# A two-layer decoder trunk on one core: other SBUF places for the operands of the split matmuls

## What is computed

```python
x = x + 0.5 * swiglu(rms_norm(x, ffn1_norm), w_gate, w_up, w_down)      # D_FF = 2816
h = rms_norm(x, mix_norm)
qa, ka, va, c_q, c_kv, k_r, g_a, g_b = split(h @ w_in)
o_a = swa_attention(qa, ka, va, ...)        # 8 heads of 64, window 128, (256, 512)
o_b = mla_attention(c_q, c_kv, k_r, ...)    # 8 heads, low-rank q and kv, (256, 512)
merged = sigmoid(g_a) * (o_a @ w_branch_a) + sigmoid(g_b) * (o_b @ w_branch_b)
x = x + merged @ w_out
x = x + 0.5 * swiglu(rms_norm(x, ffn2_norm), w_gate2, w_up2, w_down2)
```

## Time and profile before

| | |
|---|---|
| Median of 2 runs | 1044.32 us (1044.23 to 1044.41) |
| Profiled execution, whole | 1044.65 us |
| its span, first to last instruction | 1042.9 us |
| Instructions | 15577, of them 5656 matmuls |
| PE busy | 1038.1 us |
| PEld, DVE, ACT, POOL busy | 897.9, 718.1, 585.8, 62.6 us |
| Granted TensorE clock | 1.000 |
| Read from HBM | 186.04 MB, 179 GB/s over the span |

### The profile page before, as it was taken

One profiled execution on the slowest core, in us unless ns is written; L12 is line 12 of the kernel. 1 busy time (PEld: TensorE's weight loads), 2 busy tenths in 40 slices (PEclk: granted clock), 3 DMA queues, 4 the chain that ended last, 5 costly groups with the idle time before them and its releaser, 6 DMA issues.

```text
span 1042.9 us, 15577 instructions
## 1 busy us (share of the span) xinstructions
PE 1038.1 (100%) x5656; PEld 897.9 (86%) x5656; DVE 718.1 (69%) x1132; ACT 585.8 (56%) x935; POOL 62.6 (6%) x69
## 2 busy tenths in 40 slices
PE   9999999999999999999999999999999999999998
PEld 8888888998888888888888888889988888888887
DVE  6766666768786876666686666666688868676665
ACT  6555455466973754554565455455678646454552
POOL 1052000112100000000000000001211000000000
PEclk9999999999999999999999999999999999999999
DMA  6665544455435455655445555634454346545541
GB/s 264 244 221 185 212 167 166 135 185 183 156 122 202 162 190 192 206 185 208 178 148 205 201 184 184 210 131 151 162 202 162 121 162 220 203 161 201 191 171 61
DMA packets 35270, 187.60 MB, mean 180 GB/s; under 512 B 4497, under 2 KB 4641, under 8 KB 20129
## 3 DMA queue, kind: packets, MB, share of 16 engines
q1 hardware_dynamic: 34704, 186.03, 50.9%
q0 software_dynamic: 240, 0.53, 0.2%
q10 hardware_dynamic: 288, 0.54, 0.1%
HBM read 186.04 MB, written 1.05 MB: 179 GB/s over the span
## 4 chain that ended last, share of the span: by engine, by line
PE 99%; DMA 1%; DVE 0%; SPq 0%; ACT 0%; issue 0%
PE ps L1365 96%; PE ps L1786 1%; PE ps L1389 1%; DMA w_raw<-in_w_ffn 1%; PE ps L1815 1%; PE ps L1851 0%; PE ps L1695 0%; PE ps L1687 0%; DVE hT L1001 0%; PE ps L1413 0%; DVE x L994 0%; ACT w_hi L547 0%; SPq L312 0%; SPq L311 0%; DVE w_lo L912 0%
## 5 line engine op out<-in xcount | busy, mean ns | idle before, releaser
L1365 PE MATMUL ps<-hT,w_hi 128*128 128x512 f32 x1408 | 341.6, 391 | 0.3 <-DVE hT L1001 0.3
L1365 PEld LDWEIGHTS ps<-hT,w_hi 128*128 128x128 f32 x1408 | 259.1, 188 | 50.3 <-DVE hT L1001 0.5
L879 DVE TENSOR_TENSOR w_lo<-w_raw,w_hi 128x2048 fp32r<-128x2048 f32 x82 | 188.0, 2292 | 87.2 <-ACT w_hi L542 87.2
L1365 PEld LDWEIGHTS ps<-hT,w_lo 128*128 128x128 f32 x1408 | 180.8, 191 | 7.7 <-DVE w_lo L912 0.4
L1365 PE MATMUL ps<-hT,w_lo 128*128 128x256 f32 x1408 | 183.0, 283 | 0.0
L1365 PE MATMUL ps<-w_hi,hT 128*128 128x512 f32 (+2 forms) x576 | 174.1, 377 | 0.0
L542 ACT ACTIVATE w_hi<-w_raw 128x2048 fp32r<-128x2048 f32 x85 | 161.9, 1905 | 13.3 <-PE ps L1365 13.2
L1365 PE MATMUL ps<-w_lo,aTh 128*128 128x512 f32 x352 | 137.2, 390 | 0.0
L1365 PE MATMUL ps<-w_hi,aTl 128*128 128x512 f32 x352 | 137.0, 389 | 0.0
L1365 PE MATMUL ps<-w_hi,aTh 128*128 128x512 f32 x352 | 136.8, 390 | 0.0
L571 ACT ACTIVATE S<-ps 128x256 f32<-128x256 f32 x88 | 33.7, 383 | 159.7 <-PE ps L1365 159.7
(11 more groups left out here) (166 smaller groups left out, 958.2 us busy)
## 6 DMA issues: line engine op xcount, KB each, us to landing
w_raw<-in_w_ffn SPq DMA_DIRECT2D x85, 1024.0 KB, 5.0
w_raw<-in_w_ffn SPq DMA_DIRECT2D x92, 512.0 KB, 5.7
w_raw<-in_w_gate SPq DMA_DIRECT2D x16, 1024.0 KB, 4.9
w_raw<-in_w_proj SPq DMA_DIRECT2D x16, 592.0 KB, 4.7
w_raw<-in_w_branch SPq DMA_DIRECT2D x8, 1024.0 KB, 4.8
w_raw<-in_w_out SPq DMA_DIRECT2D x8, 1024.0 KB, 4.8
w_raw<-in_w_uq SPq DMA_DIRECT2D x4, 384.0 KB, 3.0
SG<-in_w_ffn SPq DMA_DIRECT2D x1, 1024.0 KB, 11.4
```

What stands on the lines that cost most here:

```text
L879: dve.tensor_tensor(wl_gu[b], raw_gu[b], wh_gu[b].bitcast(F32), ALU.subtract).then_inc(lo_gu.sem, 1)
L1365: return pe.matmul(dst, w, m, start=start, stop=stop, skip_group_check=True)
```

## The change

Rows of three tensors get holes, and three unused tensors stand between others, so that columns and tiles start at other byte addresses. In bytes: a column of hT goes from 2048 to 2080; a gap of 192 follows; a half of aTh takes 1280 in place of 1024; a gap of 320; a half of aTl takes 1184 in place of 1024; a gap of 192; a block of oTh and of oTl takes 1040 in place of 1024. The reads and writes cover the same elements as before. Where oTh and oTl were written as one run of 512 elements they are now written as two of 256. No instruction is added or removed.

```diff
+HT_GAP, OT_GAP = 8, 4
+AT_GAP, AT_GAP_L, ATH_GAP, ATL_GAP = 48, 80, 64, 40
...
         x = sb("x", [P, TT, D_MODEL])
-        hT = sb("hT", [P, KC, 2, SEQ], F32R)
+        hT_rows = sb("hT", [P, KC, 2 * SEQ + HT_GAP], F32R)
+        hT = hT_rows[:, :, 0:2 * SEQ].rearrange("p k (s n) -> p k s n", s=2)
         hTh, hTl = hT[:, :, 0, :], hT[:, :, 1, :]
-        aTh = sb("aTh", [P, 2, SEQ], F32R)
-        aTl = sb("aTl", [P, 2, SEQ], F32R)
+        aT_gap = sb("aT_gap", [P, AT_GAP])
+        aTh = sb("aTh", [P, 2, SEQ + ATH_GAP], F32R)[:, :, 0:SEQ]
+        aT_gap_l = sb("aT_gap_l", [P, AT_GAP_L])
+        aTl = sb("aTl", [P, 2, SEQ + ATL_GAP], F32R)[:, :, 0:SEQ]
+        oT_gap = sb("oT_gap", [P, AT_GAP])
         work = sb("work", [P, 4 * SEQ])
...
-        oTh = sb("oTh", [P, 8, SEQ], F32R)
-        oTl = sb("oTl", [P, 8, SEQ], F32R)
+        oTh = sb("oTh", [P, 8, SEQ + OT_GAP], F32R)[:, :, 0:SEQ]
+        oTl = sb("oTl", [P, 8, SEQ + OT_GAP], F32R)[:, :, 0:SEQ]
...
-                        act.activation(oTh[:, 4 * br + 2 * c:4 * br + 2 * c + 2, :].rearrange("p c n -> p (c n)"),
-                                       ps[:, c, :], ACT.Copy).then_inc(ot_hi.sem, 1)
+                        act.activation(oTh[:, 4 * br + 2 * c:4 * br + 2 * c + 2, :],
+                                       ps[:, c, :].rearrange("p (c n) -> p c n", c=2), ACT.Copy).then_inc(ot_hi.sem, 1)
...
-                        dve.tensor_tensor(oTl[:, part, :].rearrange("p c n -> p (c n)"), ps[:, c, :],
-                                          oTh[:, part, :].rearrange("p c n -> p (c n)").bitcast(F32),
-                                          ALU.subtract).then_inc(ot_lo.sem, 1)
+                        dve.tensor_tensor(oTl[:, part, :], ps[:, c, :].rearrange("p (c n) -> p c n", c=2),
+                                          oTh[:, part, :].bitcast(F32), ALU.subtract).then_inc(ot_lo.sem, 1)
```

## The result

The changed kernel takes 1060.24 us (median of 2 runs, both within 0.01 us) against 1044.32 before: a ratio of 1.0154, interval 1.0137 to 1.017. It is 16 us slower: less than 2%, but the whole interval lies above 1. The forecast was no change.

The account below looks back on a forecast made before the run. PE's matmul start-to-start distances were taken to bound the kernel. The 1042.9 us span plus 0 to 0.1 us, with the pitch term at 0, gave a forecast of 1044 us; the range ran from 1008 to 1062 us.

Parts of the forecast that it names:

- What bounds the kernel: PE, busy 1038.1 of 1042.9 us: the time is the sum of its matmuls' start-to-start distances.
- the 13.3 ns: Time per fp32r matmul beyond its columns, claimed whatever the length: 66.7 us over 5000, all that addresses could win.
- No added work, ACT and DVE at nothing: No instruction or wait added; the two-run writes of oTh and oTl taken as 0, bound 0.1 us.
- The pitch term: Effect of moved operand places on PE's 5000 fp32r matmuls: taken as 0, bounds 55 us faster to 16 us slower.
- The first test: Branch products with weights at 0 and oTh at 256 take 227 ns, like `down` with both at 0: displacement worth 0.
- The second test: Feed-forward stretches with DVE and ACT differently busy at wandering SBUF addresses: pitch 226 to 227 ns in both, so 0.
- rival A: Running matmul's reads collide with the next weight load's; separated places make it faster, 1014 or 994 us; over 2% faster: 0.26.
- Rival C: The 13.3 ns belong to swapping weights in the array: 1044 us, likeliest; shares 0.64 with the forecast.
- half gain: Half of the 13.3 ns goes: 4540 matmuls gain 6.7 ns, 30 us, 1014 us; 22 us without the 256-column ones.
- Rival B: An operand off a wide boundary costs an extra beat: 16 us at most, 1060 us; over 2% slower: 0.10.
- The sign for B: In the changed kernel's timeline, odd columns of hT would be slower than even ones; no size given.
- The sign for A: In the changed timeline, the distance of `down` falls first, while column 0 of hT keeps 227 ns.

Follow-up runs that it names:

- m2_widths: Measuring kernel without the trunk's computation: rows of 48 matmuls with other widths, places and bf16; 512 columns on 64 weight columns took 230 ns at 0 and 128.
- m1_places: Measuring kernel without the trunk's computation: 96 rows of 48 fp32r matmuls at chosen operand places; 512 columns took 227 ns with weights at 0, 233 at 128.
- by_256: Kernel before with hT columns 2304 bytes apart, aTh and aTl halves 1280, all places kept on multiples of 256 bytes: 1043.99 us, ratio 1.0001.
- ht_only: Kernel before with only the columns of hT 2080 bytes apart, the rest in place modulo 512: 1054.44 us, ratio 1.0099.
- at_only: Kernel before with only aTh and aTl moved, to 448, 192, 256 and 416: 1050.17 us, ratio 1.0059.
- ht_128: Kernel before with all of hT 128 bytes on, its columns still 2048 bytes apart: 1053.36 us, ratio 1.0087.
- lo_208: Kernel before with only the low gate and up weights moved 208 bytes on: 1039.23 us, ratio 0.9952.
- all_shifted: Kernel before with 96 bytes in front of all large tensors, so no place moves against another: 1044.09 us, ratio 1.0001.
- m3_pairs: Measuring kernel without the trunk's computation: rows of 48 matmuls, both operands' places taking turns; own agreement took 228 ns, agreement with the next 230.

## Why the prediction failed, point by point

**What bounds the kernel: right.** PE's pitch does, and only a change of pitch moved the time: the span's 15.6 us are the sum of the distances, and the waits went from 1.5 to 1.3 us. One reading on the way was too wide: the 13.3 ns do not stand "whatever the length", as m2_widths has 111.6 ns at 128 columns, 58 over them.

**No added work, ACT and DVE at nothing: right.** ACT's write of oTh should stay below 600 ns; it takes 594, for 589 before:

```profile
L810 ACT ACTIVATE oTh<-ps 128x512 fp32r<-128x512 f32 x8 | 4.7, 594 | 6.5 <-PE ps L1370 6.5
```

**The pitch term: wrong.** The step that failed is "the value that I take is 0, since the two tests that exist (0 against 256; busy neighbours) both say 0". The first test was blind: with a period of 256 bytes (m1_places, by_256) 0 and 256 are the same place, and the earlier trace rows could only show 227 ns. The text named this possibility itself, under rival A, and still counted the test for 0. The second test asks about other engines' reads, not about PE's own two. So two readings were taken as two votes, where neither had asked the question. The term, taken as 0, measured +15.5 us: 1408 wide ones at +5.3 ns, 1055 of `down` at +5.5, 864 on hT at +2.4, 264 on oT at +3.6, less 1408 narrow ones at -0.6.

**Rival C, no place matters, held likeliest: refuted** by m1_places, ht_only, at_only and ht_128.

**Rival A, the two reads meet.** Its premise was right: the grain is finer than 256 bytes, and the place of one operand against the other's counts. Its sign was wrong for the wide matmuls: agreeing places have the shortest pitch, 226.7 ns, and no other place that was tried was faster. For the narrow ones its sign was right: they gave 0.8 us in the change and 4 in lo_208, where its half gain on 1232 of them is 8, and the sweep's best row for them, 113.3 ns, is that half gain. The 13.3 ns of the wide ones did not go anywhere. What they are is still open: they do not shrink with the weight load's length at 512 columns, though they halve at 256 (m2_widths). Its support from the transposes fails too, namely that the excess is absent where the moving side goes at half rate: fp32r of 128 columns takes 111.6 ns at all three places tried, much like their 109.

**Rival B, slower.** The price, 5 ns on 3256 wide matmuls, 16 us, 1060 us, is the measured time almost exactly. The 3256 lost 4.9 ns on average, from 3.3 on hT to 5.5 in `down`. Its mechanism is refuted: with every operand 96 bytes off the boundary nothing is lost (all_shifted). That the sum fits is luck as far as is known, for its 5 ns were read from matmuls just after a pause, with their places unmoved. The argument against it holds only at unmoved places: there the loss does belong to the start of a run (in ht_only `down` settles after five), but the same size of loss becomes permanent when the places differ: whole rows of 48 in m1_places stay at 233.

**The pages.** The prediction weighed the Trainium skill, "TensorE: Matmul & The Clock Gate", Part 2: two independent read ports, so that loading weights takes nothing from the running matmul. No run here shows bandwidth taken as such. But the pitch of fp32r goes from 226.7 to 233 by places alone, so the rule is no warrant that the places of the two operands are free. The Trainium skill, same page, section "Wait — 56ns, not 53.3ns?", gives about 2.5 ns of fixed cost: the bf16 rows agree (215.9 against 213.3 of columns), those in fp32r do not (226.7, or 13.3 over).

**What would show it.** The three stretches named were the right ones: 3.62, 3.83 and 5.44 us became 3.73, 3.81 and 5.59. By the text's own measure (over 1 ns in any stretch) and by its closing clause, that a blind test of 0 against 256 would sink the argument, it is wrong. The sign for B, odd columns slower than even ones, does not stand in the sweep: with the moving operand at 32, 96 and 160 it takes 233.3, 233.3 and 234.3 ns, at 64, 128 and 192 it takes 228.9, 232.3 and 233.3. Only 64 stands out. The sign for A, that column 0 keeps 227 ns, was met where it ran alone and missed in the loop (228 and 230).

**"2% is about what a measurement can tell": wrong.** The interval around the ratio is 0.17% to either side, so the 1.5% is clear of noise.

**Cause: what is shown and what is not.** Shown: the 16 us come from fp32r matmuls of 512 columns whose moving and stationary operands stopped agreeing modulo 256 bytes, about 10 us by hT, 6 by aT and 1 by oT (each moved alone; the seams are counted twice). A constant difference is enough (ht_128), and other strides that keep the places modulo 256 cost nothing (by_256). Not shown: which reads of which two matmuls interfere, why weights within 16 bytes and a moving operand at 240 are as good as agreement (while both at 16 took 230.0), and why narrow ones prefer the opposite.

## What to carry to other kernels

For fp32r matmuls of 512 columns, place the moving operand and the weights alike modulo 256 bytes, keep that place from one matmul to the next, and pad rows by multiples of 256 bytes; a common shift by 96 bytes cost nothing. Where 256-column matmuls come in long runs, try the weights at another place: it brought 2 to 3 ns on each. Before a place, a stride or a phase is priced at nothing, ask whether the two cases that the trace offers could be the same case; a row of 48 matmuls for each value, many in one kernel, settles it in one run.

## What was not expected of the hardware

- The pitch of fp32r matmuls depends on the operands' places with a period of 256 bytes: 226.7 ns where they agree (but 230.0 with both at 16, and up to 234 where a common place moves on with each matmul), 229 to 235 at most of the places where they don't (512 columns). Weights 16 bytes off are free with the moving operand at 0; 4 bytes off cost 5.7 ns, and a moving operand 4 bytes off 10.
- The dependence turns with the length: 256 columns take 120.0 ns at agreeing places and 113.3 with the moving operand at 16, 112 or 192 (m3_pairs); 128 columns and bf16 show none at the places tried.
- fp32r costs 13.3 ns over its columns at agreeing places of 512, bf16 2.5. With narrower stationary tiles (96, 64, 32 columns) fp32r of 512 columns is slower, 230 to 232 ns, not faster; 256 columns on a tile of 64 are faster, 113.3 ns for 120.0.
- The same relation of places settled at different pitches (119.9 and 117.2 ns at weights 240, 256 columns; 117.8 and 116.6 at 224): PE's steady pitch seems to depend on what ran before it.
